# Feed-forward in products of pairs: sums, partial results and the gate tile in PSUM, feature sums inside the first tiles

## The chip, the cores and the metric

One core of a Trainium2 chip runs the kernel. The metric is the device time of one execution in microseconds, as the median of some runs; one further execution is recorded by the hardware profiler, and all rows below come from it.

## The reference

Two stacks of two layers each over x of 512 tokens by 1024 features, in float32. Attention and recurrent mixers alternate, and four feed-forwards close the layers. All four are of one form, with 2816 hidden features:

```python
g, u = jnp.split(h @ w_gu, 2, axis=-1)      # h: normed x
return (jax.nn.silu(g) * u) @ w_down
```

## The kernel before

Everything is feature-major: 8 tiles of 128 features by 512 tokens. A product in float32 is made of three fast ones: each operand is split into a high part (a copy rounded to fp32r, by ScalarE) and a low part (the difference), and TensorE adds high by high, low by high and high by low in a PSUM bank. Weights come as chunks of 128 by 1024 in a ring of four slots (w_raw); ScalarE writes w_hi (L1365), GpSimd writes w_lo (L625), and SP loads the next chunk of a slot when the low part is done (lo_ready).

Of the 22 hidden tiles of a feed-forward the first two are ordinary ("classic", stage gu: four output tiles, up and gate in turn, L744 to L746). The other 20 are computed as **pairs**: up and gate tile of one hidden tile together, with 7 products in place of 8, in the Strassen-Winograd manner. The two halves of the features (k and k + 4), the two halves of the tokens and up and gate make the 2 by 2 by 2 scheme. A product is 4 x 3 matmuls of 128 by 256 (L1137, L1139, L1141). Products 2, 3, 4, 6 take **feature sums** t_hi, t_lo, made once per feed-forward from x (combine, L2079 to L2086 on VectorE; combined_high L1495 on ScalarE; combined_low L2091 on VectorE; gain_part L1491 gives a scaled half of x). Products 2 to 5 take **weight sums**, made on VectorE for each pair (sum_weights: product 3 at L2108, 4 at L2111, 2 at L2113, 5 at L2116) into w_sum in SBUF. Their high parts are ScalarE's (L1349), the low parts GpSimd's (L671), but that of product 5 VectorE's (L2125).

Products of a pair go to banks a, b, c: 0 to a, 1 to b, 2 added to a, 3 to c, 4 to a, 5 to c, 6 to a. Between them ScalarE copies a partial result out to ev (copy_part, L1536: bank a after product 0, a after 2, c after 3), as an engine can't take both inputs from PSUM; product 2, 4 and 5 wait for one of these copies each. VectorE adds: b + ev (L2195) into up, a + ev (L2203) into the gate, c + ev (L2206) into up; then it multiplies by rstd (the norm): L2208 half of the gate, L2210 all of up, L2212 the other half of the gate straight from bank a when product 6 is done. ScalarE does SiLU (L1542), VectorE the product (L2163), ScalarE its high part hh (L1549), VectorE its low part hl (L2171), for pair p within the body of pair p + 1. Pairs alternate between banks 4, 5, 6 and three of banks 0 to 3.

A feed-forward has parts a, b, c with 6, 8 and 6 pairs; after each, stage dn multiplies the hidden tiles by the down weights into 8 output tiles. Each engine's order is written out by hand, as the body of a pair on VectorE:

```python
ahead(3); ahead(4)            # weight sums of the next pair
done(1); copied(0)            # L2195
ahead(2); ahead(5)
hidden_product(pair - 1, i); hidden_low(pair - 1, i)
done(4); copied(2)            # L2203
done(5); copied(1)            # L2206, L2208, L2210
done(6)                       # L2212
low_of_sum(name, pair + 1, i) # L2125
```

and on ScalarE: copy of a, high part 0 of the next pair, SiLU, high part 1, copy of a, high part 2, hidden high part, copy of c, high parts 3 to 6. All waits are on semaphores that count.

In the first two feed-forwards the feature sums are made in the loop that ends out_e and out_o (residual_out, L2254 to L2259 and L1707 to L1711), together with the addition to x (L2247), the sum of squares (L1923) and the features' low part (publish, L1930). In the last two they are made in gu, before the evictions of its tiles (L2134 to L2141), and the first pair's weight sums in the loop of xo (copies_out).

## Time and profile before

| | us |
|---|---|
| median of 3 runs | 2943.77 (2942.05 to 2945.72) |
| profiled execution | 2939.47 |
| its span | 2937.7 |

The span runs from the first to the last instruction. Busy times of engines are shares of it; a wait's row names the engine that waited, what it waited for, and the sum, count and longest in us. TensorE's rows are matmuls whose ends are modelled, so its starts are what one reads.

### The profile page before, as it was taken

What the parts mean: (1) busy time and instruction counts of PE and PEld (TensorE: products, weight loads), DVE (VectorE), ACT (ScalarE), POOL (GpSimd) and SP (SyncE); (2) the same over time, 40 slices, a digit from 0 to 9 for tenths busy, and PEclk for the clock granted to TensorE, in tenths of its full rate; (3) what the DMA queues carried; (4) which work ended last, traced back from release to release, by engine and by line L of the source; (5) the groups of instructions that cost most, each with busy time, mean ns of one, the idle gap of its engine ahead of it and who ended that gap; (6) DMA issues with size and microseconds to landing.
All of it is one profiled execution on the core that took longest, in us unless ns stands there. A gap on an engine that the chain in (4) does not pass through costs nothing.

```text
span 2937.7 us, 46989 instructions
## 1 busy us (share of the span) xinstructions
PE 2710.1 (92%) x16306; PEld 2362.0 (80%) x16306; DVE 1758.5 (60%) x2721; ACT 1351.5 (46%) x2426; POOL 1588.4 (54%) x1033
## 2 busy tenths in 40 slices
PE   9998898989999898999999997989899999789997
PEld 7767888888867888888878876888888878688886
DVE  6775748467455757555545347484757633766664
ACT  7664434346574434343255334343447533443443
POOL 4653656664453666565446335565654453466663
PEclk9999999999999999999999998999999999899998
DMA  4301122223302222232214111222222341122312
GB/s 169 108 2 58 65 101 86 92 102 104 101 16 68 81 91 93 88 110 90 97 51 148 61 65 58 91 81 101 101 93 93 113 138 51 44 101 72 108 66 86
DMA packets 69276, 252.78 MB, mean 86 GB/s; under 512 B 7680, under 2 KB 7936, under 8 KB 68864
## 3 DMA queue, kind: packets, MB, share of 16 engines
q1 hardware_dynamic: 68112, 247.43, 24.5%
q10 hardware_dynamic: 1008, 3.28, 0.3%
q8 instruction: 96, 1.57, 0.2%
q14 instruction: 60, 0.49, 0.1%
HBM read 248.58 MB, written 2.10 MB: 85 GB/s over the span
## 4 chain that ended last, share of the span: by engine, by line
PE 65%; DVE 18%; issue 10%; ACT 5%; POOL 1%; DMA 1%; DVEq 0%; ACTq 0%; SPq 0%; POOLq 0%
PE ps L744 13%; PE ps L745 13%; PE ps L746 13%; PE ps L1137 5%; PE ps L1141 4%; PE ps L1139 4%; PE ps L911 3%; PE ps L949 2%; DVE w_sum L2113 2%; DVE w_sum L2108 2%; DVE tmpb L2163 2%; DVE w_lo L2125 2%; PE ps L934 1%; DVE w_sum L2111 1%; DVE tmpb L2195 1%
## 5 line engine op out<-in xcount | busy, mean ns | idle before, releaser
L625 POOL TENSOR_TENSOR w_lo<-w_raw,w_hi 128x1024 fp32r<-128x1024 f32 x300 | 731.3, 2445 | 734.3 <-ACT w_hi L1365 723.4
L671 POOL TENSOR_TENSOR w_lo<-w_raw,w_hi 128x512 fp32r<-128x512 f32 x240 | 360.8, 1519 | 204.9 <-ACT w_hi L1349 204.9
L1365 ACT ACTIVATE w_hi<-w_raw 128x1024 fp32r<-128x1024 f32 x302 | 316.8, 1055 | 308.4 <-PE ps L746 227.7
L671 POOL TENSOR_TENSOR w_lo<-w_sum,w_hi 128x512 fp32r<-128x512 f32 x240 | 332.0, 1400 | 225.1 <-ACT w_hi L1349 225.1
L744 PE MATMUL ps<-xh,w_hi 128*128 128x512 f32 x980 | 390.5, 398 | 24.6 <-DVE xl L1930 14.3
L1137 PE MATMUL ps<-xh,w_hi 128*128 128x256 f32 x960 | 289.3, 301 | 128.1 <-ACT ev L1536 120.1
L1137 PE MATMUL ps<-t_hi,w_hi 128*128 128x256 f32 x1280 | 373.2, 292 | 21.8 <-POOL w_lo L671 20.2
L745 PE MATMUL ps<-xl,w_hi 128*128 128x512 f32 x980 | 383.3, 391 | 0.0
L746 PE MATMUL ps<-xh,w_lo 128*128 128x512 f32 x980 | 383.1, 391 | 0.0
L1139 PE MATMUL ps<-t_lo,w_hi 128*128 128x256 f32 x1280 | 371.7, 290 | 0.0
L1141 PE MATMUL ps<-t_hi,w_lo 128*128 128x256 f32 x1280 | 370.5, 289 | 0.0
L1349 ACT ACTIVATE w_hi<-w_sum 128x512 fp32r<-128x512 f32 x320 | 190.7, 625 | 272.6 <-DVE w_sum L2113 128.7
L1137 PEld LDWEIGHTS ps<-xh,w_hi 128*128 128x128 f32 x960 | 193.5, 202 | 142.7 <-ACT ev L1536 119.5
L1141 PE MATMUL ps<-xh,w_lo 128*128 128x256 f32 x960 | 282.7, 294 | 0.0
L1139 PE MATMUL ps<-xl,w_hi 128*128 128x256 f32 x960 | 282.3, 294 | 0.0
L744 PE MATMUL ps<-hh,w_hi 128*128 128x512 f32 x704 | 275.5, 391 | 4.9 <-DVE hl L2171 4.9
L1137 PEld LDWEIGHTS ps<-t_hi,w_hi 128*128 128x128 f32 x1280 | 257.3, 201 | 22.5 <-POOL w_lo L671 20.5
L745 PE MATMUL ps<-hl,w_hi 128*128 128x512 f32 x704 | 274.1, 389 | 0.0
L746 PE MATMUL ps<-hh,w_lo 128*128 128x512 f32 x704 | 274.0, 389 | 0.0
L1139 PEld LDWEIGHTS ps<-t_lo,w_hi 128*128 128x128 f32 x1280 | 256.6, 201 | 0.0
L1141 PEld LDWEIGHTS ps<-t_hi,w_lo 128*128 128x128 f32 x1280 | 255.5, 200 | 0.0
L744 PEld LDWEIGHTS ps<-xh,w_hi 128*128 128x128 f32 x980 | 185.3, 189 | 73.0 <-DVE xl L1930 16.5
(340 smaller groups left out, 5762.8 us busy)
## 6 DMA issues: line engine op xcount, KB each, us to landing
w_raw<-weights_in SPq DMA_DIRECT2D x462, 512.0 KB, 3.3
x<-x_in SPq DMA_DIRECT2D x4, 512.0 KB, 7.8
mem<-mem_in ACTq DMA_DIRECT2D x2, 1024.0 KB, 4.8
x_out<-x SPq DMA_DIRECT2D x4, 512.0 KB, 2.6
rope<-rope_in SPq DMA_DIRECT2D x1, 512.0 KB, 10.5
tab<-tables_in ACTq DMA_DIRECT2D x2, 256.0 KB, 2.8
tab<-tables_in SPq DMA_DIRECT2D x1, 384.0 KB, 11.0
small<-small_in ACTq DMA_DIRECT2D x1, 326.5 KB, 4.9
```

The lines of the kernel that those rows point to most:

```text
L625: nc.gpsimd.tensor_tensor(w_lo[:, slot], w_raw[:, slot], w_hi.bitcast(f32)[:, slot], ALU.subtract).then_inc(lo_ready, 1)
L671: last = nc.gpsimd.tensor_tensor(quad(w_lo, name, q), src, quad(w_hi, name, q).bitcast(f32), ALU.subtract)
L744: nc.tensor.matmul(dst, w_hi[:, slot, w], hi, start=first, stop=False)
L745: nc.tensor.matmul(dst, w_hi[:, slot, w], lo, start=False, stop=False)
L746: return nc.tensor.matmul(dst, w_lo[:, slot, w], hi, start=False, stop=last)
L911: last = nc.tensor.matmul(ps[:, S_BANKS[(n0 + a) % 3], cols], q, k, start=c == 0, stop=c == parts - 1)
L949: last = nc.tensor.matmul(ps[rows, g["bank"], tokens(column)], values[kb], pt[:, (n + a) % 4, tokens(sg["at"] // P + kb)], start=sg["opens ...
L1137: nc.tensor.matmul(dst, quad(w_hi, name, q)[:, w], hi, start=begins and k == 0, stop=False, skip_group_check=True)
L1139: nc.tensor.matmul(dst, quad(w_hi, name, q)[:, w], lo, start=False, stop=False, skip_group_check=True)
L1141: last = nc.tensor.matmul(dst, quad(w_lo, name, q)[:, w], hi, start=False, stop=k == 3, skip_group_check=True)
L1349: A(quad(w_hi, name, q), src, ACT.Copy).then_inc(hi_ready, 1)
L1365: A(w_hi[:, s], w_raw[:, s], ACT.Copy).then_inc(hi_ready, 1)
```

## The change

- Weight sums of products 2 and 5 go to PSUM banks 4 and 5, those of 3 and 4 stay in SBUF. VectorE makes both low parts of the former, GpSimd five low parts per pair. ScalarE's high part of sum 2 waits until sum 5 is made.
- b + ev and c + ev are written back to their banks and then multiplied by rstd into up, each half by itself. The gate tile lies in bank 6 or 7 from its first addition to its split: SiLU, product, high and low part read it there.
- Banks a, b, c of all pairs come from 0 to 3: b and c are the same for each pair, a alternates. TensorE waits for them by new counts.
- ScalarE copies c before the hidden tile's high part.
- Feature sums are made within gu in all four feed-forwards, between evictions and the first pair's weight sums; SiLU, product and split of the second classic tile go into the body of the first pair.

The diff without lines that only rename or count anew:

```diff
-w_sum = place("w_sum", [P, 4, T], 96)
+w_sum = place("w_sum", [P, 2, T], 96)
...
-SUM_OF = {2: 0, 3: 1, 4: 2, 5: 3}
...
+SUM_OF = {3: w_sum[:, 0], 4: w_sum[:, 1], 2: ps[:, 4, :], 5: ps[:, 5, :]}
+ADDED = {"b": 1, "up0": 2, "a": 3, "c": 4, "up1": 5, "gate0": 6}
...
 def pair_banks(name, pair):
-    if pair % 2 == 0:
-        return 4, 5, 6
...
-    return tuple((r + 1 + i) % RING for i in range(3))
+    return (r + 3 * (pair % 2)) % RING, (r + 1) % RING, (r + 2) % RING
+def gate_bank(pair):
+    return ps[:, 6 + pair % 2, :]
...
         def body(pair, i):
...
-                if q == 5:
+                if q in (2, 5):
...
+                src = SUM_OF[q] if q in SUM_OF else raw(name, pair, q == 6, q != 0)
...
+            def bank_free(bank):
+                before = {"a": (2, "gate0"), "b": (1, "up0"), "c": (1, "up1")}[bank]
+                pe.wait_ge(ev_added, pair_at(6 * (g - before[0]) + ADDED[before[1]] + EV_FIRST, i, 6))
+                if pair == 0:
+                    pe.wait_ge(evac_done, BANK0[name] - {"a": 3, "b": 2, "c": 1}[bank])
+                if pair == 1 and bank == "a":
+                    pe.wait_ge(evac_done, BANK0[name])
...
             low_ready(0)
-            added(4 * (g - 2) + 4)
-            if pair == 1:
-                pe.wait_ge(evac_done, BANK0[name])
+            bank_free("a")
             product_of(0, "a", True)
             low_ready(1)
-            added(4 * (g - 2) + 1)
+            bank_free("b")
             product_of(1, "b", True)
-            low_ready(2)
-            pe.wait_ge(ev_copied, pair_at(3 * g + 1, i, 3))
+            low_of_sum_ready(1)
+            copied(1)
             product_of(2, "a", False, combined if pair == 0 else None)
             low_ready(3)
-            added(4 * (g - 2) + 3)
+            bank_free("c")
             product_of(3, "c", True)
             low_ready(4)
-            pe.wait_ge(ev_copied, pair_at(3 * g + 2, i, 3))
+            copied(2)
             product_of(4, "a", False)
...
-            pe.wait_ge(ev_copied, pair_at(3 * g + 3, i, 3))
+            low_of_sum_ready(2)
+            copied(3)
             product_of(5, "c", False)
...
-            added(4 * g + 2)
+            pe.wait_ge(ev_added, pair_at(6 * g + ADDED["a"] + EV_FIRST, i, 6))
             product_of(6, "a", False)
...
-            n = 4 * g + {3: 1, 4: 2, 2: 3, 5: 4}[q]
+            n = 4 * g + {3: 1, 4: 2, 2: 4, 5: 4}[q]
...
+        src = SUM_OF[q] if q in SUM_OF else raw(name, pair, q == 6, q != 0)
...
-            act.wait_ge(tl_ready, n_.tl.n + k - 1)
+            act.wait_ge(tf_ready, n_.tl.n + k - 1)
...
+        if name not in TOGETHER:
+            high(c0 + LEAD)
+        combined_high(0)
+        gain_part(2, gname)
+        combined_high(1)
+        gain_part(3, gname)
+        if name in TOGETHER:
+            root_rows()
+            high(c0 + LEAD + 1)
+        else:
+            root()
+            high(c0 + LEAD + 1)
+        combined_high(2)
+        combined_high(3)
...
-            if j == 0 and name in TOGETHER:
-                combined_high(0)
-                gain_part(2, f"ffn_pre{f - 2}")
-                root_rows()
-                combined_high(1)
-                gain_part(3, f"ffn_pre{f - 2}")
-                high(c0 + LEAD + 1)
-                combined_high(2)
-                combined_high(3)
-            elif j == 0:
-                high(c0 + LEAD)
-                high(c0 + 1 + LEAD)
-                root()
-            else:
+            if j:
...
-            A(tmpa[:, j % 2], tmpa[:, j % 2], ACT.Silu).then_inc(silu_ready, 1)
...
-            A(hh[:, j, :], tmpb[:, j % 2], ACT.Copy).then_inc(hh_ready, 1)
+            if j < CLASSIC - 1:
+                classic_silu(f, j)
+                classic_high(j)
+    def classic_silu(f, j):
...
+        A(tmpa[:, j % 2], tmpa[:, j % 2], ACT.Silu).then_inc(silu_ready, 1)
+    def classic_high(j):
...
+        A(hh[:, j, :], tmpb[:, j % 2], ACT.Copy).then_inc(hh_ready, 1)
     def pairs(f, part):
...
         def silu(pair, i):
...
-            A(tmpa[:, pair % 2], tmpa[:, pair % 2], ACT.Silu).then_inc(silu_ready, 1)
+            act.wait_ge(ev_added, pair_at(6 * g + ADDED["gate0"] + EV_FIRST, i, 6))
+            A(gate_bank(pair), gate_bank(pair), ACT.Silu).then_inc(silu_ready, 1)
         def hidden_high(pair, i):
...
-            A(dst, tmpb[:, pair % 2], ACT.Copy).then_inc(hh_ready, 1)
+            A(dst, gate_bank(pair), ACT.Copy).then_inc(hh_ready, 1)
         def body(pair, i):
...
             if pair:
...
+            elif part == "a":
+                classic_silu(f, CLASSIC - 1)
             ahead(1)
             copy_part(pair, i, 1, 2, "a")
             ahead(2)
+            copy_part(pair, i, 2, 3, "c")
+            ahead(3)
             if pair:
                 hidden_high(pair - 1, i)
-            copy_part(pair, i, 2, 3, "c")
-            for q in range(3, QUADS):
+            elif part == "a":
+                classic_high(CLASSIC - 1)
+            for q in range(4, QUADS):
                 ahead(q)
...
             publish(m, gname)
-            if m >= 4:
-                gain_part(m - 4, gname)
-            if m >= 5:
-                combined_high(m - 5)
-        combined_high(3)
+        gain_part(0, gname)
+        gain_part(1, gname)
...
-    def sums_of_first(name):
-        for which in (3, 4, 2, 5):
-            sum_weights(name, 0, which)
...
+    def sums_of_first(name, which=(3, 4, 2, 5)):
+        for q in which:
+            sum_weights(name, 0, q)
+    def low_of_sum(name, pair, q, i=None):
+        dve.wait_ge(hi_ready, pair_at(product_done(name, pair, q), i, QUADS))
+        V.tensor_tensor(quad(w_lo, name, q), SUM_OF[q], quad(w_hi, name, q).bitcast(f32),
...
     def gate_up(f):
...
-        for j in range(CLASSIC):
-            for q, dst in ((0, tmpb), (1, tmpa)):
-                m = 2 * j + q
-                if m == 0 and f >= 2:
-                    gname = f"ffn_pre{f - 2}"
-                    combine(0, gname)
-                    combined_low(0)
-                    inverse_rms_kept(1e-6)
-                    for k in range(1, 4):
-                        combine(k, gname)
-                        combined_low(k)
-                dve.wait_ge(chunk_done, DONE[c0 + m])
-                if m == 0 and f < 2:
-                    inverse_rms(rstd, 1e-5)
-                scaled(dst[:, j % 2], ps[:, (g0 + m) % 4, :]).then_inc(evac_done, 1)
-            if j == 0 and f < 2:
-                sums_of_first(f"pairs{f}a")
...
-            V.tensor_tensor(tmpb[:, j % 2], tmpa[:, j % 2], tmpb[:, j % 2],
-                            ALU.mult).then_inc(prod_ready, 1)
...
-            V.tensor_tensor(hl[:, j, :], tmpb[:, j % 2], fp(hh)[:, j, :], ALU.subtract).then_inc(hl_ready, 1)
...
+        def evict(m):
+            dve.wait_ge(chunk_done, DONE[c0 + m])
+            scaled((tmpa if m % 2 else tmpb)[:, m // 2], ps[:, (g0 + m) % 4, :]).then_inc(evac_done, 1)
+        combine(0, gname)
+        combine(1, gname)
+        combined_low(0)
+        if f < 2:
+            inverse_rms(rstd, 1e-5)
+        else:
+            inverse_rms_kept(1e-6)
+        combine(2, gname)
+        combined_low(1)
+        sums_of_first(first, (3, 4))
+        evict(0)
+        evict(1)
+        combine(3, gname)
+        combined_low(2)
+        sums_of_first(first, (2, 5))
+        combined_low(3)
+        classic_product(0)
+        low_of_sum(first, 0, 2)
+        classic_low(0)
+        evict(2)
+        evict(3)
+        low_of_sum(first, 0, 5)
+    def classic_product(j):
...
+        V.tensor_tensor(tmpb[:, j % 2], tmpa[:, j % 2], tmpb[:, j % 2], ALU.mult).then_inc(prod_ready, 1)
+    def classic_low(j):
...
+        V.tensor_tensor(hl[:, j, :], tmpb[:, j % 2], fp(hh)[:, j, :], ALU.subtract).then_inc(hl_ready, 1)
     def pairs(f, part):
...
         def hidden_product(pair, i):
...
-            V.tensor_tensor(tmpb[:, pair % 2], tmpa[:, pair % 2], tmpb[:, pair % 2],
+            V.tensor_tensor(gate_bank(pair), gate_bank(pair), tmpb[:, pair % 2],
...
         def hidden_low(pair, i):
...
-            V.tensor_tensor(at(hl), tmpb[:, pair % 2], at(fp(hh)), ALU.subtract).then_inc(hl_ready, 1)
+            V.tensor_tensor(at(hl), gate_bank(pair), at(fp(hh)), ALU.subtract).then_inc(hl_ready, 1)
         def body(pair, i):
...
-            up, gate = tmpb[:, pair % 2], tmpa[:, pair % 2]
+            up, gate = tmpb[:, pair % 2], gate_bank(pair)
...
+            def low_ahead(q):
+                if not last:
+                    low_of_sum(name, pair + 1, q, i)
...
-            def added(ins):
...
+            def added(what):
+                dve.wait_ge(ev_added, pair_at(6 * g + ADDED[what] + EV_FIRST, i, 6))
...
             done(1)
             copied(0)
-            added(V.tensor_tensor(up[:, first], b, ev[:, 0], ALU.add))
+            V.tensor_tensor(b, b, ev[:, 0], ALU.add).then_inc(ev_added, 1)
             ahead(2)
+            added("b")
+            V.tensor_tensor(up[:, first], b, rstd[:, first], ALU.mult).then_inc(ev_added, 1)
             ahead(5)
             if pair:
                 hidden_product(pair - 1, i)
-                hidden_low(pair - 1, i)
+            elif part == "a":
+                classic_product(CLASSIC - 1)
             done(4)
             copied(2)
-            added(V.tensor_tensor(gate[:, second], a, ev[:, 2], ALU.add))
+            V.tensor_tensor(gate[:, second], a, ev[:, 2], ALU.add).then_inc(ev_added, 1)
+            low_ahead(2)
+            if pair:
+                hidden_low(pair - 1, i)
+            elif part == "a":
+                classic_low(CLASSIC - 1)
             done(5)
             copied(1)
-            added(V.tensor_tensor(up[:, second], c, ev[:, 1], ALU.add))
-            dve.wait_ge(ev_added, pair_at(4 * g + 2 + EV_FIRST, i, 4))
+            V.tensor_tensor(c, c, ev[:, 1], ALU.add).then_inc(ev_added, 1)
+            added("a")
...
-            dve.wait_ge(ev_added, pair_at(4 * g + 3 + EV_FIRST, i, 4))
-            V.tensor_tensor(up, up, rstd[:], ALU.mult)
+            added("c")
+            V.tensor_tensor(up[:, second], c, rstd[:, second], ALU.mult).then_inc(ev_added, 1)
             done(6)
-            added(V.tensor_tensor(gate[:, first], a, rstd[:, first], ALU.mult))
-            if not last:
-                low_of_sum(name, pair + 1, i)
-            else:
+            V.tensor_tensor(gate[:, first], a, rstd[:, first], ALU.mult).then_inc(ev_added, 1)
+            low_ahead(5)
+            if last:
...
-        low_of_sum(name, 0)
+        if part != "a":
+            low_of_sum(name, 0, 2)
+            low_of_sum(name, 0, 5)
...
-            if m >= 5:
-                combine(m - 5, gname)
-                combined_low(m - 5)
...
-        combine(3, gname)
-        combined_low(3)
...
-            if m == KT - 2:
-                sums_of_first(then)
...
```

## Rows read from the trace of the kernel before

**Rows 1.** The page: busy time of each engine and its share of the span
```profile
PE 2710.1 (92%) x16306; PEld 2362.0 (80%) x16306; DVE 1758.5 (60%) x2721; ACT 1351.5 (46%) x2426; POOL 1588.4 (54%) x1033
```
**Rows 2.** Waits of TensorE: total us, times, longest us
```profile
PE ps L1137 <- ACT ev L1536: 120.1, 67, 2.4
PE ps L1137 <- POOL w_lo L671: 28.0, 4, 10.5
PE ps L744 <- DVE xl L1930: 14.3, 5, 4.4
PE ps L744 <- DVE hl L2171: 4.9, 4, 1.2
```
**Rows 3.** Stretches of pairs: us, busy us (count) by engine, PEclk, DMA share, GB/s
```profile
2668.80:2767.60 98.80, 86.79 (x674) 85.39 (x673) 79.88 (x98) 48.30 (x91) 67.42 (x46) 0.95 0.26 91
...
sum 1010.70, PE 868.63 PEld 854.54 DVE 798.65 ACT 497.09 POOL 678.60; mean PE 72.39 PEld 71.21 DVE 66.55 ACT 41.42 POOL 56.55
```
**Rows 4.** Timeline of TensorE: start, us, what, and in brackets idle time before it
```profile
438.89 0.36 PE L1137 MATMUL ps<-xh,w_hi 128*128 128x256 f32 x1 [0.33 <-ACT ev L1536]
451.56 0.39 PE L1137 MATMUL ps<-xh,w_hi 128*128 128x256 f32 x1 [2.37 <-ACT ev L1536]
464.15 0.39 PE L1137 MATMUL ps<-xh,w_hi 128*128 128x256 f32 x1 [2.26 <-ACT ev L1536]
```
**Rows 5.** Timeline of VectorE in the same pair, and one slower sum 2
```profile
436.37 1.44 DVE L2113 SCALAR_TENSOR_TENSOR w_sum<-w_sum,w_raw 128x512 f32<-128x512 f32 x1
...
455.46 0.41 DVE L2212 TENSOR_TENSOR tmpa<-ps,rstd 128x256 f32<-128x256 f32 x1
455.79 1.56 DVE L2125 TENSOR_TENSOR w_lo<-w_sum,w_hi 128x512 fp32r<-128x512 f32 x1
457.28 1.80 DVE L2108 SCALAR_TENSOR_TENSOR w_sum<-w_raw 128x512 f32<-128x512 f32 x1
459.01 1.78 DVE L2111 TENSOR_TENSOR w_sum<-w_raw 128x512 f32<-128x512 f32 x1
...
461.05 0.68 DVE L2113 SCALAR_TENSOR_TENSOR w_sum<-w_sum,w_raw 128x512 f32<-128x512 f32 x1
461.76 0.69 DVE L2116 TENSOR_TENSOR w_sum<-w_raw,w_sum 128x512 f32<-128x512 f32 x1
462.37 0.68 DVE L2163 TENSOR_TENSOR tmpb<-tmpa,tmpb 128x512 f32<-128x512 f32 x1
```
**Rows 6.** Timeline of ScalarE: the copy of bank c
```profile
463.73 0.37 ACT L1536 ACTIVATE ev<-ps 128x256 f32<-128x256 f32 x1
```
**Rows 7.** Groups on VectorE: count, busy us, mean ns, idle before
```profile
L2206 DVE TENSOR_TENSOR tmpb<-ps,ev 128x256 f32<-128x256 f32 x80 | 34.0, 426 | 99.1 <-PE ps L1141 99.1
L2208 DVE TENSOR_TENSOR tmpa<-tmpa,rstd 128x256 f32<-128x256 f32 x80 | 70.5, 881 | 0.0
```
**Rows 8.** Stretches by engine: a stage dn, and 3.41 us behind a wait
```profile
387.50:431.30 43.80, 43.80 (x195) 36.02 (x194) 12.87 (x15) 9.92 (x13) 21.97 (x11) 1.00 0.25 84
477.25:480.66 3.41, 3.41 (x18) 3.41 (x18) 1.61 (x5) 1.11 (x2) 2.52 (x2) 0.51 0.00 0
```
**Rows 9.** Timeline of TensorE in the first tile of the first gu
```profile
287.28 0.50 PE L744 MATMUL ps<-xh,w_hi 128*128 128x512 f32 x1 [2.14 <-DVE xl L1930]
292.60 0.80 PE L744 MATMUL ps<-xh,w_hi 128*128 128x512 f32 x1 [4.36 <-DVE xl L1930]
```
**Rows 10.** Groups on VectorE: reciprocal, low part of a feature sum, one of its operations
```profile
L1968 DVE RECIPROCAL rstd<-tmpb 128x512 f32<-128x512 f32 x6 | 20.1, 3353 | 7.0 <-ACT tmpb L1408 7.0
L2091 DVE TENSOR_TENSOR t_lo<-t_f,t_hi 128x1024 fp32r<-128x1024 f32 x16 | 19.6, 1226 | 18.0 <-ACT t_hi L1495 18.0
L2079 DVE SCALAR_TENSOR_TENSOR t_f<-x,small,x_f 128x256 f32<-128x256 f32 x16 | 7.7, 478 | 0.1
```
**Rows 11.** Timeline of TensorE at the first pair of the third feed-forward
```profile
1773.90 0.39 PE L1137 MATMUL ps<-xh,w_hi 128*128 128x256 f32 x1 [3.92 <-POOL w_lo L671]
1788.98 0.55 PE L1137 MATMUL ps<-t_hi,w_hi 128*128 128x256 f32 x1 [10.45 <-POOL w_lo L671]
```

54 lines of the change are left out of this document (25 added, 29 removed).

## The prediction

> **What bounds the kernel now.** I read the shares of the page first: TensorE is busy 92% of the span, VectorE 60% [rows 1]. So only TensorE's idle time and the time in which it runs slower can be won. The waits by engine say where the idle time is [rows 2]: 120.1 us in 67 waits of L1137 (the products of the pairs) for L1536, ScalarE's copies of a partial result into ev; 28.0 us in 4 waits for GpSimd's low parts of the weights, all at the first pair of a feed-forward; 14.3 us for L1930, the low part of the features; 4.9 us for the last hidden tile. A table of the 12 stretches of pairs (6, 8 and 6 in each of four feed-forwards) gives 1010.7 us [rows 3]. The time from one resumption of TensorE to the same place a pair later is 464.15 - 451.56 = 12.59 us, 2.26 of them idle [rows 4], so a pair is 10.33 us of work. 80 of them are 826 us: the stretches hold 184 us that aren't work.
>
> What ends that wait is a chain through two engines. TensorE's product 5 wants the copy of bank c, which ScalarE makes after L1549 (high part of the hidden tile), which waits for L2163, which VectorE reaches only after all four weight sums [rows 5, 6]. VectorE starts L2212 when product 6 is done (455.46), then low part of sum 5 (1.56), sum 3 (1.80), sum 4 (1.78), addition of b, sum 2 (0.68), sum 5, hidden product (462.37 to 463.05) [rows 5]; ScalarE follows with L1549 and at 463.73 with the copy, and TensorE resumes at 464.15: 8.7 us. VectorE is also some 0.65 us late for product 6, as L2208 and L2210 stand before it. The sums take 1.8 us where others take 0.68: they wait for GpSimd, whose L671 holds the second read of SBUF. An addition of 256 columns with one operand in PSUM takes 426 ns on average, the same shape with both in SBUF 881 [rows 7].
>
> **The change in the pairs.** VectorE: L2210 (one of 512 columns) becomes two multiplications of 256 (0.41 each), a low part of 512 columns comes over from GpSimd (sum 2), the rest keeps its count. That is 0.4 + 0.7 = 1.1 us more instructions per pair. GpSimd has five low parts for six. Operations with an operand in PSUM are taken at the price of [rows 7], so both low parts, the product, L2171, and the gate's multiplication no longer wait for GpSimd. For sum 2 (still two SBUF inputs, output now in PSUM) there are two rows, 0.68 and 1.44 us [rows 5]. I take 1.4, since GpSimd's lows 0 and 1 of the next pair fall there, and keep 0.7 for the range. Bounds of an operation from PSUM to PSUM are those of the two groups of [rows 7].
>
> ScalarE: the copy of c now stands before the hidden tile, behind only the high part of sum 2; that one waits for all four sums. The new chain from product 6 done: L2212 0.34, low part of sum 5 0.60, sum 3 1.6, sum 4 1.7, addition of b 0.34, sum 2 1.4, first multiplication 0.34, sum 5 0.69, ScalarE's high part 0.55 and copy 0.4, which is 8.0. The 0.65 of lateness goes, as the multiplication that stood before L2212 is now short. From resumption to product 6 done are two products (2 x 10.33 / 7) and 0.35 until VectorE sees it: 3.3. So the next period is 3.3 + 8.0 = 11.3 us, against 12.6. The wait stays, on the same copy, with about 1.0 us of idle time in place of 2.3; what is late next is sum 5.
>
> - 56 pairs have the full wait (80, less 12 last ones, which sum nothing ahead, and 12 first ones): 56 x 1.3 = **-73 us**.
> - The 8 first pairs of the later parts wait 0.33 us now [rows 4] and will wait some 1.0: **+5 us**. The extra order between sums (two weights for bank 4 and 5) has no other price.
> - The clock. In 477.25 to 480.66, right after a wait, TensorE has half its clock (0.51; 1.2 of 2.4 GHz) [rows 8]. Over the stretches PEclk is 0.95 on average, which is some 30 such spells of 3.4 us; 20 of them lie outside the heads. Each costs 1.7 us, of which about half only shortens the next wait. With waits of 1.0 us I expect them to vanish: 20 x 0.85 = **-17 us**.
> - The banks: b is now the same for each pair and its multiplication comes right behind sum 2, five products before it is wanted; at nothing. If that cover is gone, the price is product 1 waiting, at most VectorE's 1.4.
> - The end of a part: less stands before the last hidden tile; of the 4.9 us [rows 2], **-4 us**.
>
> **Feature sums.** They leave the loops of out_e and out_o. There VectorE's part of a tile is longer than TensorE's, and the two waits of 2.14 and 4.36 us that come of it [rows 9] go: 2 x 6.5 = **-13 us**. In their place VectorE has four feature sums within gu, each four operations of 0.48 and a low part of 1.23 [rows 10]. Added up from 3.6 us behind gu's start: two feature sums 3.6 and 2.3 of waiting for GpSimd's L625, a low part 1.2, the norm 5.6 (0.6, ScalarE's root 1.6, reciprocal 3.4 [rows 10]), feature sum and low part 2.9, two weight sums and two evictions 2.4, feature sum and low part 2.9, two weight sums 1.3, low part 1.2, product 0.7: 27.7. Behind it ScalarE makes the hidden high part, five high parts of 0.53 and the first copy: 31.3. TensorE, at 43.8 us for 8 tiles [rows 8], has done gu's four and two products at about 26. That is 5 to 6 us of wait where there is about 1, and product 5 of pair 0, behind four sums that start late, waits some 4 for 2.1: 2 x 6.5 = **+13 us**. So this move is even in the first two feed-forwards.
>
> In the last two the sums are already there, and the waits are 3.92 (product 0) and 10.45 us (product 2) [rows 11, 2]. ScalarE's gain parts wait for less, so the high part of product 0 is early, but bank a now needs the first eviction, which stands behind the third feature sum and two weight sums: 2.9 us in place of 3.9. Product 2 comes 39 us behind gu's start for 45. Product 5 gives 3.3 back. 2 x (6.0 - 3.3) = 5.4, and VectorE no longer makes four weight sums ahead of the last copy of xo: between 0 and 2.7 us each time (four by 0.68), I take 1.0, as ScalarE's square ends there at about the same time. **-7 us**. No DMA is added or moved, and SP waits for lo_ready as before, so its queue counts for nothing; the weights of pair 0 are read later than now.
>
> Sum: -73 + 5 - 17 - 4 - 13 + 13 - 7 = -96 us, against the profiled execution's 2939.47 (span 2937.7): 2843. The median of the runs, 2943.77, is 4.3 above that execution, so 2847.
>
> A rule speaks against keeping the gate tile in PSUM through multiplication, SiLU, product, split. The rows first: 512 columns with both inputs in SBUF and unhindered take 0.68 or 0.69 us (L2113, L2116), as L2163 does, and what comes from PSUM has the same rate (426 ns for 256), so PSUM costs nothing here. The Trainium skill, VectorE: DVE Perf Modes, "Rules for kernel authors", advises to copy a matmul's output to SBUF first when many operations follow. By it one copy per pair would pay; by the rows it would add 0.7 us of VectorE to a chain that sets the pace, 64 x 0.7 = 45 us.
>
> **The rivals.**
> 1. The sums meet no wait. If sum 2 takes 0.7 and sum 3 half its wait, the period falls to TensorE's 10.33: 64 x 0.95 = 60 us more, **2787**. For it: GpSimd has 5 low parts. Against: they follow the same high parts. 0.12.
> 2. The wait stays whole: the high part of sum 2 now waits for sum 5 too, and the move of the copy gives nothing back. Then -73, -17 and +5 fall away: **2932**. Against it is that L1549 alone is 0.53 and L2163 0.6 of the old chain. 0.15.
> 3. Slower: VectorE becomes the bound, because operations with an operand in PSUM wait for GpSimd like the others where GpSimd runs. Then the low part of sum 5 is 1.5, the first multiplication 0.9, the lateness stays: 3.3 + 8.0 + 0.9 + 0.5 + 0.65 = 13.35, 0.75 above now in 68 pairs: +51, nothing from the clock, heads -11: **2984**. It decides from a chain of 9.3 us on. Against it is the group of 426 ns. The Trainium skill (SBUF — State Buffer, "Who interferes with whom") says that only an instruction with two SBUF inputs contends; by that rule, this rival is out, and the trace's groups agree. 0.09.
>
> **How the numbers follow.** The forecast has 0.64. Its own range: sum 2 at 0.7 gives -45, sums 3 and 4 at 1.8 each give +15, the heads +-15: 2800 to 2880. The range for 8 in 10 reaches to rival 1 and most of the way to rival 2: 2785 to 2920. 0.2% is 6 us, about what a measurement of this kernel can tell from no change. Faster by more: the forecast, rival 1 and most of rival 2, 0.89; within: 0.03; slower: 0.08.
>
> **What would show it.** A pair's period of 11.3 in the middle of a part, product 5 still waiting for ev, about 1 us; low parts of the sums at 0.69 on VectorE; sum 2 near 1.4; PEclk 1.0 in the stretches of 8 pairs; no wait of L744 for L1930; 5 to 6 us before product 2 in the first two feed-forwards, 7 in the others. It is wrong if product 1 or 3 waits for a bank, if low parts from PSUM take over 1 us, or if the first pair's wait grows beyond 10 us.

## The result, and the profile after

The changed kernel takes 2813.99 us (median of 4 runs, 2812.47 to 2815.52), the kernel before 2943.15 in the same measurement: a ratio of 0.956, 95% interval 0.9543 to 0.9577. That is 129 us less where the prediction had 96 less, 2847 in a range from 2785 to 2920. The profiled execution of the changed kernel took 2812.47, its span 2810.6, against 2939.47 and 2937.7 before.

First the page: busy time by engine, the span in 40 slices, then two of TensorE's waits that are left and answer to [rows 2] (L1140 is what L1137 was).

```profile
PE 2669.9 (95%) x16306; PEld 2328.5 (83%) x16306; DVE 1705.8 (61%) x2881; ACT 1335.0 (47%) x2426; POOL 1444.9 (51%) x953
...
PEclk9999999999999999999999999999999999999998
...
PE ps L1140 <- ACT ev L1557: 55.0, 65, 1.7
PE ps L1140 <- issue: 22.3, 4, 6.8
```

VectorE has 53 us less busy time for 160 more instructions: it waits less for GpSimd, which has 80 instructions fewer. The wait for the copy in ev is there in 65 places, 67 before, but 55 us in all where it was 120. The 28.0 us for GpSimd's L671 and 13.0 of the 14.3 for the features' low part [rows 2] are gone; in their place are 22.3 us in 4 waits put down to "issue", which are product 2 of the four first pairs, and 4.8 us in 2 waits ahead of product 0 in the last two feed-forwards.

The 12 stretches of pairs, by the same view as [rows 3] (us, busy us and count for PE, PEld, DVE, ACT, POOL, then PEclk, DMA share, GB/s): a first part, a second and a third of one feed-forward, the last second part, and the sum over all twelve.

```profile
303.64:377.68 74.04, 64.16 (x505) 63.05 (x504) 64.16 (x94) 41.31 (x77) 44.08 (x31) 0.95 0.26 93
421.23:509.26 88.03, 82.38 (x674) 80.99 (x673) 76.15 (x114) 46.89 (x91) 54.18 (x39) 1.00 0.29 102
552.80:618.61 65.81, 61.72 (x506) 60.73 (x505) 55.38 (x84) 34.88 (x67) 40.52 (x29) 1.00 0.30 105
...
2561.67:2649.71 88.04, 82.38 (x674) 80.99 (x673) 76.16 (x114) 46.88 (x91) 54.19 (x39) 1.00 0.29 102
...
sum 911.75, PE 834.45 PEld 820.87 DVE 782.41 ACT 492.21 POOL 556.41; mean PE 69.54 PEld 68.41 DVE 65.20 ACT 41.02 POOL 46.37
```

The stretches give back 1010.7 - 911.8 = 98.9 us of the 127.1 by which the span became shorter. The clock is 1.00 in the second and third parts, where it was 0.93 to 0.98 before (0.95 in the one that [rows 3] shows); it is below 1 only in the first parts, which hold the long wait of the first pair.

One pair on VectorE and ScalarE, and TensorE's resumption at the end of it; it answers to [rows 4, 5, 6].

```profile
454.91 0.43 DVE L2261 TENSOR_TENSOR ps<-ps,rstd 128x256 f32<-128x256 f32 x1 [0.26 <-PE ps L1144]
455.25 0.68 DVE L2148 TENSOR_TENSOR w_lo<-ps,w_hi 128x512 fp32r<-128x512 f32 x1
455.85 1.67 DVE L2131 SCALAR_TENSOR_TENSOR w_sum<-w_raw 128x512 f32<-128x512 f32 x1
457.44 1.81 DVE L2134 TENSOR_TENSOR w_sum<-w_raw 128x512 f32<-128x512 f32 x1
459.18 0.42 DVE L2236 TENSOR_TENSOR ps<-ps,ev 128x256 f32<-128x256 f32 x1
459.51 1.45 DVE L2136 SCALAR_TENSOR_TENSOR ps<-w_sum,w_raw 128x512 f32<-128x512 f32 x1
460.88 0.41 DVE L2239 TENSOR_TENSOR tmpb<-ps,rstd 128x256 f32<-128x256 f32 x1
461.21 0.68 DVE L2139 TENSOR_TENSOR ps<-w_raw,ps 128x512 f32<-128x512 f32 x1
```
```profile
461.93 0.60 ACT L1361 ACTIVATE w_hi<-ps 128x512 fp32r<-128x512 f32 x1 [2.24 <-DVE ps L2139]
462.42 0.38 ACT L1557 ACTIVATE ev<-ps 128x256 f32<-128x256 f32 x1
```

Here is the whole chain of the prediction, instruction by instruction: gate multiplication, low part of sum 5, sums 3 and 4, addition of b, sum 2, first up multiplication, sum 5, high part of sum 2, copy of bank c. TensorE takes up product 5 at 462.85, 7.94 us behind 454.91 (8.0 was forecast), after 0.78 us of idle time (1.0 forecast), and 11.11 us behind the same place of the pair before (11.3 forecast, 12.6 before).

### The profile page after: what moved, and what is told of

Read it like the earlier page. It is cut to its first block, busy times and chain, and to the rows that moved or that the text cites. A ratio compares the mean times of both kernels' runs of the same rounds, so it can differ in the third digit from the quotient of the medians.

```text
span 2810.6 us, 47222 instructions
## 1 busy us (share of the span) xinstructions
PE 2669.9 (95%) x16306; PEld 2328.5 (83%) x16306; DVE 1705.8 (61%) x2881; ACT 1335.0 (47%) x2426; POOL 1444.9 (51%) x953
## 4 chain that ended last, share of the span: by engine, by line
PE 72%; DVE 14%; issue 8%; ACT 4%; DVEq 0%; DMA 0%; POOL 0%; ACTq 0%; SPq 0%; POOLq 0%
PE ps L747 14%; PE ps L749 14%; PE ps L748 14%; PE ps L1140 6%; PE ps L1144 6%; PE ps L1142 6%; PE ps L914 3%; DVE w_sum L2131 2%; PE ps L952 2%; PE ps L937 2%; DVE ps L2139 1%; ACT ev L1557 1%; PE ps L856 1%; DVE w_sum L2134 1%; PE ps L858 1%
## 5 line engine op out<-in xcount | busy, mean ns | idle before, releaser
L674 POOL TENSOR_TENSOR w_lo<-w_raw,w_hi 128x512 fp32r<-128x512 f32 x240 | 348.1, 1465 | 169.4 <-ACT w_hi L1361 169.4
L1140 PE MATMUL ps<-t_hi,w_hi 128*128 128x256 f32 x1280 | 367.3, 287 | 22.3 <-issue 22.3
L674 POOL TENSOR_TENSOR w_lo<-w_sum,w_hi 128x512 fp32r<-128x512 f32 x160 | 208.0, 1319 | 299.9 <-ACT w_hi L1361 299.9
L1140 PE MATMUL ps<-xh,w_hi 128*128 128x256 f32 x960 | 278.6, 290 | 59.8 <-ACT ev L1557 55.0
L1144 PE MATMUL ps<-xh,w_lo 128*128 128x256 f32 x960 | 272.3, 284 | 0.0
L1142 PE MATMUL ps<-xl,w_hi 128*128 128x256 f32 x960 | 272.1, 283 | 0.0
L1140 PEld LDWEIGHTS ps<-t_hi,w_hi 128*128 128x128 f32 x1280 | 250.5, 196 | 23.1 <-issue 23.1
L1142 PEld LDWEIGHTS ps<-t_lo,w_hi 128*128 128x128 f32 x1280 | 250.5, 196 | 0.0
L1140 PEld LDWEIGHTS ps<-xh,w_hi 128*128 128x128 f32 x960 | 184.2, 192 | 73.8 <-ACT ev L1557 50.7
L747 PEld LDWEIGHTS ps<-xh,w_hi 128*128 128x128 f32 x980 | 185.2, 189 | 57.4 <-issue 10.9
L749 PEld LDWEIGHTS ps<-xh,w_lo 128*128 128x128 f32 x980 | 184.9, 189 | 39.3
## 6 DMA issues: line engine op xcount, KB each, us to landing
tab<-tables_in SPq DMA_DIRECT2D x1, 384.0 KB, 11.3
```

What stands on the lines that cost most here:

```text
L674: last = nc.gpsimd.tensor_tensor(quad(w_lo, name, q), src, quad(w_hi, name, q).bitcast(f32), ALU.subtract)
L747: nc.tensor.matmul(dst, w_hi[:, slot, w], hi, start=first, stop=False)
L749: return nc.tensor.matmul(dst, w_lo[:, slot, w], hi, start=False, stop=last)
L1140: nc.tensor.matmul(dst, quad(w_hi, name, q)[:, w], hi, start=begins and k == 0, stop=False, skip_group_check=True)
L1142: nc.tensor.matmul(dst, quad(w_hi, name, q)[:, w], lo, start=False, stop=False, skip_group_check=True)
L1144: last = nc.tensor.matmul(dst, quad(w_lo, name, q)[:, w], hi, start=False, stop=k == 3, skip_group_check=True)
```

## The experiments

Each row below is the median of four runs beside the kernel before on the same chip, which took 2944.3 to 2945.7 there. "Changed" is 2814, with the kernel before at 2943.2; so a difference of 2 us between two rows says nothing.

| run | edit | us |
|---|---|---|
| e1_copy_first | changed, copy of c ahead of the high part of sum 2 | 2743.5 |
| e2_copy_last | changed, copy of c behind the hidden tile's high part | 2858.1 |
| e3_sum5_first | changed, sum 5 ahead of the first up multiplication | 2800.4 |
| e4_before_copy | before, copy of c ahead of the hidden tile's high part | 2922.6 |
| e5_gate_sbuf | changed, gate tile in SBUF | 2844.5 |
| e6_heads | e1, and another order of the first pair | 2736.4 |
| e7_sums_upstream | changed, feature sums of two feed-forwards moved back | 2814.3 |
| e8_weight_sums_sbuf | changed, weight sums 2 and 5 in SBUF | 2845.0 |
| e9_sums_split | e6, feature sums of two feed-forwards split | 2743.2 |
| e10_up_sbuf | changed, up tile's partial results in SBUF | 2802.0 |

**e1: the copy ahead of the high part of sum 2.**

```diff
-                    ahead(2)
                     copy_part(pair, i, 2, 3, "c")
+                    ahead(2)
                     ahead(3)
```

> The changed kernel with one edit on ScalarE: bank c's partial result (product 3) is copied ahead of the high part of sum 2 instead of behind it. Theory A (the one wait left in a pair, 0.78 us ahead of product 5, hangs on the chain gate multiplication, sums 3, 4, 2, 5 on VectorE, high part of sum 2, copy on ScalarE): product 3 is done some 1.5 us before that high part can begin, so the copy is ready long before product 5, the wait is gone, and the next bound is TensorE's own 10.2 us or VectorE's 11.12 less its 0.60 idle = 10.5 us a pair: 0.6 to 0.9 us x 56 pairs = 35 to 50 us less than the changed kernel, 2764 to 2779. Theory B (VectorE's load with its waits for GpSimd is the bound, and product 5 only shows it): the wait comes back ahead of product 6 or of product 2 of the next pair at nearly its size, 2800 to 2814.

Measured: 2743.48 (2741.48 to 2746.63), ratio to before 0.9317 (0.9301 to 0.9332): 70 us less than the changed kernel, more than theory A's 35 to 50. The second part of the first feed-forward:

```profile
417.40:498.00 80.60, 80.60 (x673) 80.56 (x672) 72.97 (x114) 46.99 (x91) 54.21 (x38) 1.00 0.32 111
```

TensorE has no idle time at all in 8 pairs, 10.08 us each, and its list of waits has no entry for ev any more. I had a floor of 10.5 from VectorE, 11.12 less its idle 0.60. That floor isn't one, as sum 3 shows:

```profile
439.16 1.33 DVE L2131 SCALAR_TENSOR_TENSOR w_sum<-w_raw 128x512 f32<-128x512 f32 x1
...
443.71 0.38 ACT L1557 ACTIVATE ev<-ps 128x256 f32<-128x256 f32 x1 [1.06 <-PE ps L1144]
444.89 0.60 ACT L1361 ACTIVATE w_hi<-ps 128x512 fp32r<-128x512 f32 x1 [0.79 <-DVE ps L2139]
```

The copy is made 1.2 us before the high part can begin, and sum 3 takes 1.33 where it took 1.67. The duration of sum 3 holds waiting time for GpSimd, and it shrinks when VectorE runs ahead of GpSimd (1.22 us on average for 1.43; sum 4 keeps its 1.70). So the wait that the prediction left in each pair was there by the order of two instructions on ScalarE alone. Theory A holds, with its size off; B falls.

The size is read from the stretches. A period is 10.08 us for 11.12, 1.04 less, though the wait that went is only 0.78: TensorE's part of a pair is 10.34 us with the wait in it and 10.08 without, so the 10.33 that the prediction took for a pair's work holds some 0.25 us that belong to the wait. 56 periods are 58 us of the 70; the rest is mostly the waits of the first pairs at product 5, 0.92 to 1.67 us, which went too.

**e2: the copy where it was.**

```diff
                     ahead(2)
-                    copy_part(pair, i, 2, 3, "c")
-                    ahead(3)
                     if pair:
                         hidden_high(pair - 1, i)
                     elif part == "a":
                         classic_high(CLASSIC - 1)
+                    copy_part(pair, i, 2, 3, "c")
+                    ahead(3)
```

> The changed kernel with the one edit on ScalarE undone: the copy of bank c's partial result stands behind the hidden tile's high part again, as in the kernel before. Theory A: this high part waits for the product that VectorE makes behind sum 5 (0.69 us) and takes 0.5 to 0.6 itself, so the copy ends 0.6 to 0.7 us later in each of 56 pairs: 34 to 40 us more than the changed kernel, 2848 to 2854. Theory B: where ScalarE's order carries nothing, since VectorE sets the pace, 2814 to 2820.

Measured: 2858.14 (2856.49 to 2859.25), 44 us more than the changed kernel: theory A, 4 us above its range. The wait list has it, 43 us more in 68 waits:

```profile
PE ps L1140 <- ACT ev L1557: 98.2, 68, 3.1
```

So 44 of the 129 us hang on this one edit, once the rest of the change is there.

**e4: the copy moved in the kernel before.**

```diff
                     ahead(2)
+                    copy_part(pair, i, 2, 3, "c")
+                    ahead(3)
                     if pair:
                         hidden_high(pair - 1, i)
-                    copy_part(pair, i, 2, 3, "c")
-                    for q in range(3, QUADS):
+                    for q in range(4, QUADS):
```

> The kernel before with the ScalarE edit alone: the copy of bank c's partial result ahead of the hidden tile's high part. Theory A, by the chain: the copy no longer waits for the hidden tile's product, but on VectorE the hidden tile's low part still stands ahead of the addition into bank a, and it waits for ScalarE's high part, now one copy later: the wait leaves product 5 and comes back ahead of product 6, and the time is within 5 us of the kernel before. Rival: the copy alone carries the gain of the whole change, 1 us or more a pair, 2880 or less.

Measured: 2922.56 (2922.07 to 2927.53), ratio 0.9923 (0.9907 to 0.994); 23 us less by the medians, 12 by the two profiled executions. TensorE's waits:

```profile
PE ps L1137 <- DVE tmpa L2204: 65.0, 68, 2.1
PE ps L1137 <- ACT ev L1536: 56.3, 67, 2.1
```

The wait moves as theory A has it, but not pair by pair. In the middle of a part 2.26 us ahead of product 5 have become 0.86 there and 0.73 ahead of product 6, and a period is 12.2 us for 12.6; the last pair of each part, which met no wait of this kind before, now has 1.98 us ahead of product 6:

```profile
462.74 0.39 PE L1137 MATMUL ps<-xh,w_hi 128*128 128x256 f32 x1 [0.86 <-ACT ev L1536]
465.17 0.39 PE L1137 MATMUL ps<-t_hi,w_hi 128*128 128x256 f32 x1 [0.73 <-DVE tmpa L2204]
...
526.26 0.55 PE L1137 MATMUL ps<-t_hi,w_hi 128*128 128x256 f32 x1 [1.98 <-DVE tmpa L2204]
```

The two nearly cancel, and so 120.1 us in one wait [rows 2] are 121.3 in two. What the forecast of no more than 5 us missed is the clock. In the pairs of the kernel before there are 41 waits of 2.06 to 2.37 us. Behind 25 of them the granted clock was 0.50 to 0.64, as in [rows 8] behind the wait that ended at 476.74; behind the other 16 it was 1.00, the one of 464.15 [rows 4] among them. In this run it was 1.00 behind all 114 waits of 0.6 to 1.0 us, and low behind 6 of the 14 of 1.98 to 2.07. First the kernel before, then this one:

```profile
464.15:467.55 3.40, 3.40 (x28) 3.40 (x29) 2.48 (x5) 1.84 (x4) 2.57 (x3) 1.00 0.00 0
```
```profile
462.74:466.14 3.40, 2.67 (x20) 2.46 (x21) 2.45 (x6) 2.25 (x4) 3.40 (x3) 1.00 0.00 0
```

In the second and third parts the clock took some 16 us before and takes 3 here (worked out as in the table further down); that is the gain. So about the same idle time in sum cost less in shorter pieces. And the two parts of the change need each other: 23 us for the copy alone, 44 with the rest.

**e3: sum 5 ahead of the first up multiplication.**

```diff
                     ahead(2)
+                    ahead(5)
                     added("b")
                     V.tensor_tensor(up[:, first], b, rstd[:, first], ALU.mult).then_inc(ev_added, 1)
-                    ahead(5)
```

> The changed kernel with sum 5 ahead of the up tile's first multiplication on VectorE instead of behind it. Theory A: the multiplication's 0.33 us leaves the chain, ScalarE's high part of sum 2 begins 0.33 us sooner: 0.33 x 56 = 18 us less than the changed kernel, 2795 to 2800, and the wait ahead of product 5 is 0.45 us where it was 0.78. Theory B: no change, 2814, since VectorE's work is the same in sum.

Measured: 2800.44 (2798.04 to 2804.19), 14 us less. Theory A by its sign, with 0.2 us a pair for the 0.33 that left the chain: a stretch of 8 pairs takes 86.65 us for 88.03, over 7 periods. VectorE shows the rest:

```profile
459.83 1.46 DVE L2136 SCALAR_TENSOR_TENSOR ps<-w_sum,w_raw 128x512 f32<-128x512 f32 x1
461.33 0.70 DVE L2139 TENSOR_TENSOR ps<-w_raw,ps 128x512 f32<-128x512 f32 x1
```

From sum 2 to what follows it are 1.50 us here and 460.88 - 459.51 = 1.37 in the changed kernel. Sum 5 reads what sum 2 writes, and the program has it wait for sum 2's semaphore; it begins only when sum 2 is done. The multiplication between them had hidden 0.13 us of that.

**e10: the up tile's partial results in SBUF.**

```diff
-                    V.tensor_tensor(b, b, ev[:, 0], ALU.add).then_inc(ev_added, 1)
+                    V.tensor_tensor(up[:, first], b, ev[:, 0], ALU.add).then_inc(ev_added, 2)
                     ahead(2)
-                    added("b")
-                    V.tensor_tensor(up[:, first], b, rstd[:, first], ALU.mult).then_inc(ev_added, 1)
...
-                    V.tensor_tensor(c, c, ev[:, 1], ALU.add).then_inc(ev_added, 1)
+                    V.tensor_tensor(up[:, second], c, ev[:, 1], ALU.add).then_inc(ev_added, 1)
...
-                    V.tensor_tensor(up[:, second], c, rstd[:, second], ALU.mult).then_inc(ev_added, 1)
+                    V.tensor_tensor(up, up, rstd[:], ALU.mult).then_inc(ev_added, 1)
```

> The changed kernel with the up tile's partial results added into SBUF and multiplied there in one instruction of 512 columns at the end, as before; the sums into the gate tile stay in PSUM. Theory A (the chain from product 6 to the copy ahead of product 5 sets the period): the first up multiplication, 0.33 us, leaves the chain; the one of 512 columns, all in SBUF, meets GpSimd's low parts and takes 1.3 us or more where two of 256 took 0.33 each, but it stands where VectorE has 0.26 us to spare and, if it ends late, the sum behind it waits less for GpSimd: between 18 us less and 20 us more than the changed kernel, 2796 to 2834. Theory B (each operation freed of its wait for GpSimd is worth its wait): the 1 us more in each of 56 pairs shows in full, 2860 or more.

Measured: 2801.96 (2798.58 to 2803.4), 12 us less than the changed kernel, so this part of the change cost time. The groups on VectorE, the multiplication of 512 columns and sum 3:

```profile
L2131 DVE SCALAR_TENSOR_TENSOR w_sum<-w_raw 128x512 f32<-128x512 f32 x80 | 92.8, 1160 | 0.0
L2259 DVE TENSOR_TENSOR tmpb<-tmpb,rstd 128x512 f32<-128x512 f32 x80 | 87.1, 1088 | 0.0
```

The multiplication takes 1.09 us for two of 0.41, but sum 3, behind it, takes 1.16 where it took 1.43: the wait for GpSimd is met once, by whoever comes first. What is left is the 0.33 that leaves the chain, less the 0.13 of sum 5 right behind sum 2, as in e3, with the same 86.67 us for 8 pairs.

**e5: the gate tile in SBUF.**

```diff
         def gate_bank(pair):
-            return ps[:, 6 + pair % 2, :]
+            return tmpa[:, pair % 2]
```

> The changed kernel with the gate tile in SBUF throughout, as before: only its bank of PSUM is given up. Theory A (an operation of VectorE with all its operands in SBUF waits for a GpSimd operation that is running, one with an operand in PSUM does not): the hidden tile's low part meets GpSimd's two low parts and takes 1.3 to 1.8 us instead of 0.69, the two gate multiplications may wait too; VectorE has 0.26 us to spare before product 6 is done, so a pair becomes 0.4 to 1.0 us longer: 22 to 56 us more than the changed kernel, 2836 to 2870. Theory B (the skill's rule taken at its word: work on PSUM costs more than work on SBUF): 2814 or less, with the product and the low part shorter than 0.69 us.

Measured: 2844.52 (2843.94 to 2847.68), 31 us more. The size is theory A's, the place isn't: 8 pairs take 88.12 us against 88.03. On VectorE the low part and the second gate multiplication are longer and sum 3 shorter, with the same end. The time is lost behind the pairs, where TensorE's list has a new entry, 12 waits at the ends of the 12 parts. The eight stages behind a first or second part take 45.2 us for 43.6, with a wait of 1.3 each; behind a third part the wait is 2.7, and behind the one that ended at 626.72 the clock was 0.50 for 3.40 us, which is part of the 10 us that the list doesn't hold:

```profile
PE ps L747 <- DVE hl L2208: 21.4, 12, 2.7
```

In the last pair of a part no weight sum follows that could take up a delay. There VectorE's operations run beside GpSimd's low parts of the next stage's weights, of 2.4 us each:

```profile
373.89 2.48 DVE L2208 TENSOR_TENSOR hl<-tmpa,hh 128x512 fp32r<-128x512 f32 x1
...
376.63 2.28 DVE L2257 TENSOR_TENSOR tmpa<-tmpa,rstd 128x256 f32<-128x256 f32 x1
```
```profile
373.42 2.41 POOL L628 TENSOR_TENSOR w_lo<-w_raw,w_hi 128x1024 fp32r<-128x1024 f32 x1 [0.54 <-PE ps L1144]
376.09 2.54 POOL L628 TENSOR_TENSOR w_lo<-w_raw,w_hi 128x1024 fp32r<-128x1024 f32 x1 [0.26 <-ACT w_hi L1377]
```

They end 0.5 and 0.3 us behind the end of the GpSimd operation that they met. In the changed kernel the same low part reads PSUM, begins inside a GpSimd operation, and takes 0.69:

```profile
375.41 0.69 DVE L2208 TENSOR_TENSOR hl<-ps,hh 128x512 fp32r<-128x512 f32 x1
```
```profile
374.97 2.41 POOL L628 TENSOR_TENSOR w_lo<-w_raw,w_hi 128x1024 fp32r<-128x1024 f32 x1 [0.69 <-PE ps L1144]
```

**e8: weight sums 2 and 5 in SBUF.**

```diff
-        w_sum = place("w_sum", [P, 2, T], 96)
+        w_sum = place("w_sum", [P, 4, T], 96)
...
-        SUM_OF = {3: w_sum[:, 0], 4: w_sum[:, 1], 2: ps[:, 4, :], 5: ps[:, 5, :]}
+        SUM_OF = {3: w_sum[:, 0], 4: w_sum[:, 1], 2: w_sum[:, 2], 5: w_sum[:, 3]}
```

> The changed kernel with weight sums 2 and 5 in SBUF instead of PSUM; who makes what in which order is as in the changed kernel. Theory A (the wait for GpSimd is met by when an operation starts, and these start where GpSimd mostly idles: sum 5 at 461.2, low parts at 455.3 and 463.2, GpSimd's operations at 455.7, 457.4 to 460.4 and 463.4): 0 to 0.3 us a pair, 2814 to 2830. Theory B (each of the three operations is freed of a wait by its bank of PSUM): sum 5 and the two low parts take 1.3 us or more, some 1.2 us a pair more, 2860 to 2890.

Measured: 2844.97 (2842.06 to 2847.49), 31 us more, which neither theory has. In the middle of a part A holds: sum 5 and both low parts take 0.67 to 0.68 there, and a period is 11.22 for 11.12. But in the first pair of a part the two low parts begin as GpSimd does, and then sum 3 waits too:

```profile
423.09 2.38 DVE L2148 TENSOR_TENSOR w_lo<-w_sum,w_hi 128x512 fp32r<-128x512 f32 x2
425.40 1.78 DVE L2131 SCALAR_TENSOR_TENSOR w_sum<-w_raw 128x512 f32<-128x512 f32 x1
```
```profile
431.82 0.38 PE L1140 MATMUL ps<-xh,w_hi 128*128 128x256 f32 x1 [2.19 <-ACT ev L1557]
```
```profile
431.82:435.22 3.40, 3.40 (x17) 3.40 (x18) 1.62 (x4) 1.48 (x3) 2.90 (x2) 0.53 0.00 0
```

In the changed kernel the two took 1.28, sum 3 took 0.88, and the wait was 0.92. In all four second parts the clock behind this wait is 0.51 to 0.56 besides; in the third parts, where the same 2.19 stand, it is 1.00. A second part takes 91.4 us for 88.0, a third part 67.5 for 65.8.

**e7: the feature sums of the first two feed-forwards back.** VectorE's part; ScalarE's follows it, and gate_up keeps the sums for the last two feed-forwards only.

```diff
                     if m:
                         publish(m - 1, gname)
+                    if m >= 5:
+                        combine(m - 5, gname)
+                        combined_low(m - 5)
                 publish(KT - 1, gname)
+                combine(3, gname)
+                combined_low(3)
```

> The changed kernel with the feature sums of the first two feed-forwards back in the stages that end in the residual, as before; the other two feed-forwards keep theirs. Theory A (by the two traces: the stages ahead became 8.9 and 10.2 us shorter, of which some 1.3 each by the last part's first product, and the first pairs lose 5.1 us each at product 2 and some at half the clock): 16 to 18 us come back ahead of the pairs, 9 to 13 leave the first pairs, 2818 to 2823. Theory B (the prediction's terms, 13 against 13): 2814.

Measured: 2814.28 (2811.36 to 2816.13), no difference: theory B, the prediction's, and A falls. Both sides are larger than the prediction had them, though. The stages ahead become 9.7 and 9.0 us longer, with TensorE's wait and the clock behind it:

```profile
293.24 0.80 PE L747 MATMUL ps<-xh,w_hi 128*128 128x512 f32 x1 [4.36 <-DVE xl L1958]
...
293.30:296.70 3.40, 3.40 (x6) 2.08 (x7) 2.24 (x5) 1.77 (x2) 0.00 (x0) 0.50 0.02 5
```

and the two first parts become 8.1 us shorter each, 65.9 and 65.8 for 74.0 and 73.9. That leaves 2.5 us, and 1.6 of them are made up ahead of the third feed-forward (477.4 us for 479.0), where this edit changes nothing.

**e6: the order of the first pair.** On top of e1. VectorE's part in gate_up is below; combine(2) and combined_low(1) went into waits of the norm ahead of it, and on ScalarE the copy of product 0 stands behind the high parts of sums 4 and 5.

```diff
-                combine(2, gname)
-                combined_low(1)
-                sums_of_first(first, (3, 4))
                 evict(0)
                 evict(1)
+                sums_of_first(first)
                 combine(3, gname)
                 combined_low(2)
-                sums_of_first(first, (2, 5))
+                low_of_sum(first, 0, 2)
                 combined_low(3)
+                evict(2)
                 classic_product(0)
-                low_of_sum(first, 0, 2)
                 classic_low(0)
-                evict(2)
                 evict(3)
```

> The kernel of the first experiment (bank c's copy early) with another order of the first pair: on VectorE the first two evictions stand right behind the reciprocal mean square, feature sum 2 and the low part of sum 1 beside the wait for the root, all weight sums in one go and the low part of weight sum 2 ahead of the last feature low part; on ScalarE the copy of product 0 stands ahead of the first hidden tile's high part. Theory A (a first pair loses 5.1 us ahead of product 2 in the first two feed-forwards, 2.4 + 6.8 in the last two, to the order of VectorE's and ScalarE's work): 3 to 5 us less in each of the first two, 5 to 8 in each of the others: 2718 to 2728 against the 2743 of the first experiment. Theory B (VectorE is full from its reciprocal on, so the wait only moves to product 6 of the first pair): 2738 to 2743.

Measured: 2736.36 (2733.15 to 2739.02), ratio 0.9286 (0.9266 to 0.9306): the lowest median of all, 7 us below e1 (whose interval, 0.9301 to 0.9332, overlaps it), between the theories and nearer to B. The 5.06 us before product 2 in the first feed-forward are 0.38, and two waits stand further back in their place:

```profile
308.84 0.35 PE L1140 MATMUL ps<-t_hi,w_hi 128*128 128x256 f32 x1 [0.38 <-issue]
314.52 0.39 PE L1140 MATMUL ps<-t_hi,w_hi 128*128 128x256 f32 x1 [2.58 <-ACT ev L1549]
319.51 0.36 PE L1140 MATMUL ps<-t_hi,w_hi 128*128 128x256 f32 x1 [0.39 <-DVE ps L2248]
```

The first parts of the first two feed-forwards are 2.4 us shorter each than in e1 (66.2 for 68.6). In the last two nothing like the 5 to 8 us of theory A came: these parts became 1.9 and 0.7 us longer, and 2.4 and 1.8 us were won ahead of them.

**e9: two feature sums ahead, two behind.** On top of e6, VectorE's part in residual_out; the other two stand at the start of gate_up.

```diff
                         publish(m - 1, gname)
+                    if m in (5, 6):
+                        combine(m - 5, gname)
+                        combined_low(m - 5)
                 publish(KT - 1, gname)
```

> The kernel of the sixth experiment with the feature sums of the first two feed-forwards split: feature sums 0 and 1 with their low parts go into the stage ahead, under its last tiles but one, where VectorE idles 3.5 us a tile; 2 and 3 stay behind the last tile, ahead of the root. Theory A (all four upstream cost 8 to 10 us there because 2 and 3 stand ahead of the last tile's low part, and all four behind it fill VectorE under the first pair; two by two they fit into idle time at both places): the stage ahead stays as short, the first two feed-forwards lose their 5.7 us in the first pair: 10 to 12 us less than the sixth experiment, 2724 to 2727. Theory B (whatever is moved upstream is paid there): 2733 to 2740.

Measured: 2743.19 (2742.14 to 2744.7), ratio 0.9317 (0.9301 to 0.9334), 7 us more than e6: theory B by its sign, 3 us above its range. The first parts lost only 2.1 us each to their first pair, 5.7 in e6, but the two stages ahead paid 9.2 us in waits for the features that e6 doesn't have. Its idle 3.5 us a tile weren't free: behind a feature sum the next tile's operations run later and meet GpSimd, as this addition does, 0.68 us when alone:

```profile
283.05 2.27 DVE L1953 TENSOR_TENSOR acc<-acc,tmpa 128x512 f32<-128x512 f32 x1
```

## Why the prediction was right in kind and a quarter too small

The terms against the two traces:

| term | forecast | measured |
|---|---|---|
| 56 pairs, period 12.6 to 11.3 | -73 | 56 x (12.60 - 11.12) = -83 |
| 8 first pairs of later parts | +5 | 8 x (8.27 - 7.68) = +5 |
| clock in the pairs | -17 | -21 |
| ends of the parts | -4 | -8 |
| stages ahead of the first two | -13 | -17 |
| first pairs of the first two | +13 | +12 |
| first pairs of the last two and what is ahead | -7 | -8 and -3 |
| periods without any wait | none | 3 x (10.1 - 11.1) = -3 |
| sum | -96 | -126 of 127 |

The measured column is worked out from the two traces. A first pair is read from the part's start to the resumption at product 5 (431.21 to 438.89 before, 421.23 to 429.50 after), a period from one such resumption to the next. The clock's row is what all parts of before hold above periods of 12.60 and 13.05 us from the last resumption to the end. The ends are eight stages dn by 0.2 us and 1.5 us behind the last pair of each of the four feed-forwards. Stages ahead go from there to the first pair's start. So the forecast's parts have the right sign everywhere, and the 30 us that it lacks are spread: 10 in the period, 3 to 4 each in five other rows.

**The period** was right link by link: the chain took 7.94 us for 8.0, with sum 3 to sum 4 at 1.59 and sum 4 to the addition at 1.74, for 1.6 and 1.7. The stretch ahead of it, from TensorE's resumption to VectorE's taking up product 6, was 3.2 for 3.3. That and rounding are the 0.18 us a pair that make -73 into -83. e2 and e3 bear two of its links out. What the prediction didn't see is that the last link but one was there by order alone; e1 found 70 us in it.

**The first pairs of later parts** wait 0.92 us where they waited 0.33, and are longer by that difference: +5, as forecast.

**The clock** was rightly said to come back where waits are near 1 us: in the changed kernel it is 1.00 behind all 65 waits for ev (0.77 to 1.67 us) and 0.50 behind the 5.07. The kernel before had 25 spells of low clock behind its waits for ev, 23 of them outside the first pairs, where the forecast counted 20, and they cost 0.85 us each, as forecast. But the prediction priced the clock only there. Behind the longer of the two waits of [rows 9] that it took for 6.5 us stand 3.40 us at 0.50 (e7 shows the same), 1.7 us each time: 3.4 of the 4 us by which the stages ahead gave more. What was mis-sized there is a stall priced by its idle time alone.

**The heads.** Product 2 waits 5.07, 5.06, 6.82 and 5.34 us, for 5 to 6 and 7 in the forecast, and product 0 in the last two 2.4 for 2.9. Wrong was "product 5 of pair 0 waits some 4": it waits 1.5 us in the first feed-forward, and at most 1.7 anywhere, since product 2 starts late and VectorE has that time. That +13 came out at +12 is luck. From the part's start to product 5 the first feed-forward takes 16.4 us for 10.4; 3.7 us of that are idle time (forecast 6.5), and 2.3 are the half clock behind the 5.07, which the prediction didn't count. In the last two feed-forwards a first pair gave back 4.1 us from the part's start on; the forecast had 2.7, with product 0's wait included. What lies ahead of them gave 3 us more than its end of a part; but these two stretches differ by up to 1.8 and 2.9 us between kernels that have the same code there (477.3 to 479.1 and 414.3 to 417.2), so that number says little. Three periods of the third feed-forward met no wait at all; why these three stays open.

**The feature sums** were forecast to be even in the first two feed-forwards. By e7 they are, with 18.7 us ahead and 16.2 in the first parts instead of 13 and 13.

**The end of a part** was put at 4 us and gave 8: the 4.9 us of waits [rows 2] are all gone, and each of the 12 stages dn is 0.2 us shorter. The gate tile's place in PSUM is worth far more there: 31 us by e5. The kernel before, with this tile in SBUF too, waited 4.9 us there [rows 2] where e5 waits 21.4; why it lost so little stays open. Which part of the gain belongs to the low part of sum 2 on VectorE and to the new banks of a, b and c stays open too: no run has the change without them.

**The rivals.** The first (no wait met, 2787) lay on the right side but needs shorter sums; the traces have them at 1.45 to 1.81. The second is refuted by e2, and the third by e5, where the same low part takes 2.48 us in SBUF and 0.69 in PSUM beside a running GpSimd operation. That agrees with the Trainium skill, SBUF — State Buffer, "Who interferes with whom", by which a VectorE instruction with two SBUF inputs contends with a GpSimd instruction that reads SBUF, and one with at most one SBUF input does not, outside the two-port modes. The advice to copy a matmul's output to SBUF first (the Trainium skill, VectorE: DVE Perf Modes, "Rules for kernel authors") does not hold here: e5 has the tile in SBUF without even paying for a copy, and is 31 us slower. The rate is no reason for it either way: with GpSimd idle the low part takes 0.69 us in SBUF too (e5, at 381.66). It is right in another sense for the up tile, where e10 gains 12 us, but through the order of the chain and not through the rate of PSUM.
